# A one-layer decoder step on one core: SyncE issues key pages ahead of value pages in each slot's turn

## The reference

```python
def fox_sample(q, k, v, logf, k_past, v_past, logf_past):
    c = jnp.cumsum(jnp.concatenate([logf_past, logf], axis=1), axis=1)
    s = jnp.concatenate([einsum('bqhd,bkhd->bhqk', q, k_past), einsum('bqhd,bkhd->bhqk', q, k)], -1) * scale
    bias = c[:, p_len:].transpose(0, 2, 1)[..., None] - c.transpose(0, 2, 1)[:, :, None, :]
    p = softmax(where(kpos <= qpos, s + bias, -inf))
    return einsum('bhqk,bkhd->bqhd', p[..., :p_len], v_past) + einsum('bhqk,bkhd->bqhd', p[..., p_len:], v)
...
k_past = cache_k[l][page_table].reshape(bs, past, FOX_HEADS, FOX_HD)
v_past = cache_v[l][page_table].reshape(bs, past, FOX_HEADS, FOX_HD)
```

## Time and profile before

| | |
|---|---|
| time, median of 3 runs (lowest, highest) | 2030.86 us (2027.76, 2032.69) |
| the profiled execution's own time | 2028.18 us |
| its span, first to last instruction | 2026.50 us |
| PE busy | 1946.4 us, 96% of the span |
| DVE, ACT, POOL busy | 56%, 32%, 10% |
| mean granted TensorE clock | 0.990 of full speed |
| cache page loads | 256 of keys and 256 of values, 256 KB each |
| median time from issue to landing of a page | 4.7 us |

### The profile page before, as it was taken

How to read it: one execution, slowest core, us unless ns; L and a number is a source line. 1 busy time by engine, 2 the same in 40 slices (tenths; PEclk the granted TensorE clock), 3 DMA queues, 4 the chain that set the end, 5 groups by cost and what they waited for, 6 DMA issues and landing times.

```text
span 2026.5 us, 37147 instructions
## 1 busy us (share of the span) xinstructions
PE 1946.4 (96%) x14259; PEld 1824.2 (90%) x14259; DVE 1144.4 (56%) x1757; ACT 644.4 (32%) x1202; POOL 196.4 (10%) x230
## 2 busy tenths in 40 slices
PE   7999999999999999989999998999999999999996
PEld 6887888988888898878899997999999999999996
DVE  6545646988877967886426758433323333243348
ACT  5434444234134133223402215433102231132334
POOL 1000000111010020020000100000000000000005
PEclk9999999999999999999999999999999999999999
DMA  5111113898997988887724310111111111111154
GB/s 160 42 43 43 42 43 100 267 309 278 320 314 243 332 284 279 296 294 249 255 80 135 91 42 22 53 42 52 42 52 42 52 39 46 51 42 52 37 158 139
DMA packets 152197, 276.66 MB, mean 137 GB/s; under 512 B 19009, under 2 KB 58702, under 8 KB 152054
## 3 DMA queue, kind: packets, MB, share of 16 engines
q1 hardware_dynamic: 116418, 175.22, 25.8%
q0 software_dynamic: 23296, 82.96, 14.0%
q10 hardware_dynamic: 12368, 16.88, 2.4%
HBM read 247.37 MB, written 27.72 MB: 136 GB/s over the span
## 4 chain that ended last, share of the span: by engine, by line
PE 77%; DVE 12%; DMA 6%; issue 2%; ACT 2%; SPq 2%; ACTq 0%; DVEq 0%; POOL 0%; POOLq 0%
PE bank L125 56%; PE bank L142 5%; PE bank L1788 3%; DMA cache_keys<-in_cache_k_dram 2%; PE bank L983 2%; PE bank L521 2%; PE bank L533 2%; DVE score L1288 2%; DVE cache_keys L1284 1%; DMA cache_vals<-in_cache_v_dram 1%; SPq L845 1%; PE banks L505 1%; PE banks L507 1%; PE banks L1079 1%; DMA x_stage<-in_x_prompt_dram 1%
## 5 line engine op out<-in xcount | busy, mean ns | idle before, releaser
L125 PE MATMUL bank<-x_hi,w_hi 128*128 128x344 f32 x1872 | 608.2, 325 | 7.6 <-DVE rot_sin L1356 3.9
L125 PE MATMUL bank<-x_hi,w_lo 128*128 128x344 f32 x1872 | 599.6, 320 | 0.0
L125 PE MATMUL bank<-x_lo,w_hi 128*128 128x344 f32 x1872 | 599.2, 320 | 0.0
L125 PEld LDWEIGHTS bank<-x_hi,w_hi 128*128 128x128 f32 x1872 | 353.7, 189 | 19.4 <-issue 8.9
L125 PEld LDWEIGHTS bank<-x_lo,w_hi 128*128 128x128 f32 x1872 | 353.3, 189 | 0.2 <-issue 0.2
L125 PEld LDWEIGHTS bank<-x_hi,w_lo 128*128 128x128 f32 x1872 | 353.5, 189 | 0.0
L101 ACT ACTIVATE w_hi<-w_raw 128x1024 fp32r<-128x1024 f32 (+3 forms) x139 | 142.1, 1023 | 380.6 <-PE bank L125 365.8
L125 PE MATMUL bank<-moving_lo,w_hi 128*128 128x344 f32 x744 | 237.5, 319 | 0.0
L125 PE MATMUL bank<-moving_hi,w_hi 128*128 128x344 f32 x744 | 223.1, 321 | 2.4 <-DVE moving_lo L1962 2.0
L108 DVE TENSOR_TENSOR w_lo<-w_raw,w_hi 128x1024 fp32r<-128x1024 f32 (+1 forms) x138 | 164.0, 1189 | 79.9 <-ACT w_hi L101 72.2
L125 PE MATMUL bank<-moving_hi,w_lo 128*128 128x344 f32 x648 | 207.1, 320 | 0.0
(11 more groups left out here) (295 smaller groups left out, 2863.7 us busy)
## 6 DMA issues: line engine op xcount, KB each, us to landing
cache_keys<-in_cache_k_dram SPq DMA_DIRECT2D x256, 256.0 KB, 4.7
cache_vals<-in_cache_v_dram SPq DMA_DIRECT2D x256, 256.0 KB, 4.7
w_raw<-in_w_in_dram POOLq DMA_DIRECT2D x52, 512.0 KB, 6.1
w_raw<-in_w_up_dram POOLq DMA_DIRECT2D x22, 512.0 KB, 4.5
w_raw<-in_w_gate_dram POOLq DMA_DIRECT2D x22, 512.0 KB, 4.6
tail_raw<-in_w_down_dram SPq DMA_DIRECT2D x22, 448.0 KB, 3.7
gate<-gate_t_scratch SPq DMA_DIRECT2D x15, 516.0 KB, 3.5
w_raw<-in_w_down_dram POOLq DMA_DIRECT2D x10, 448.0 KB, 4.4
```

Source lines behind the costliest of these rows:

```text
L125: mm = pe.matmul(g.bank[n][0:m, 0:TC], w[slot][:, k, 0:m], x[:, k, chunk(n)], start=(k == 0 and i == 0), stop=(k == kt - 1 and i == 2))
```

## The change

In `load_both` the two loads of a slot's turn change places: the key group's wait and its two pages come first, the value group's wait and its two pages behind them. The load of the value groups' page numbers moves with them, from before the first turn to between the first key group and the first value group. The functions around it, the rings, the waits' values and all other engines' programs stay as they are.

```diff
             def load_both(n, q, of, quad):
 
-                value_ids = page_ids(of, quad)
+                key_ids = page_ids(n, q)
                 for slot in range(SLOTS):
+                    load_group(keys, k_land, k_used, ck, n, q, slot, key_ids)
+                    if slot == 0:
+                        value_ids = page_ids(of, quad)
                     load_group(vals, v_land, v_used, cv, of, quad, slot, value_ids)
-                    if slot == 0:
-                        key_ids = page_ids(n, q)
-                    load_group(keys, k_land, k_used, ck, n, q, slot, key_ids)
```

## The result

| | kernel before | changed kernel |
|---|---|---|
| time, median (lowest to highest; runs) | 2030.57 us (2025.39 to 2035.04; 6) | 2044.38 us (2039.0 to 2050.28; 6) |
| ratio of the two, 95% interval | | 1.0068 (1.0054 to 1.0083) |
| the profiled execution, its span | 2028.18, 2026.5 us | 2050.28, 2048.6 us |
| mean granted TensorE clock | 0.990 | 0.981 |

The change costs 13.8 us, or 0.68%. Two executions in all, one of the kernel before timed beside runs 1 to 4 (2461.24 us) and one of run 8's kernel timed again (2380.12 us), ran at a mean granted clock of 0.72 and 0.75 and are left out of every median and ratio here. The changed kernel's profiled execution is its slowest, 5.9 us above its median. The two profiles differ by 22.1 us in span, and a share of that is not the change's, as the first windows show.

The account below looks back on a forecast made before the run. TensorE was taken to set the end of the 345 to 1000 us stretch. Terms 2.7 + 2.6 + 1.1 + 1.1 - 1.0 + 3.7 = +10.2 us, added to 2030.86, gave 2041 us, range 2034 to 2054.

Parts of the forecast that it names:

- Head 1's end: Value group 54, issued behind key group 70's wait, lands 3.3 us late near 659 us; +2.7 us, bounds to +6.0.
- the +8 that the prediction names: Approximate sum in us if a 256 KB page took 2.6 us, making groups 54 and 86 each 1.9 us late.
- Head 2's end: Value groups 86 and 89 come 3.0 and 4.8 us late, 2.15 there already; +2.6 us, bounds +0.9 and +5.6.
- Head 0, value group 8: Takes key group 24's place at 429.20 us and lands at most 1.3 us late; +1.1 us, bounds 0 and +2.0.
- The gain at 516 us: Earlier key group 39 shortens TensorE's 3.9 us wait behind VectorE's rotation; -1.0 us, bounds 0 and -1.8.
- Head 3, group 102: TensorE already waits for values here and each is issued one place later; +1.1 us, bounds 0 and +2.0.
- TensorE's clock: New stalls at 659 and 817 us drop the clock to half rate for a while; +3.7 us, bounds +1.0 and +8.0.
- the two terms named as likely to be off: If only the size was wrong, the error was expected in the clock's term or in value group 89's.
- rival 3: Much slower: TensorE's lateness feeds back through VectorE's rotations and key slots at heads 1 to 3; 2055 us, chance 0.05.
- rival 1: Faster: earlier keys make VectorE earlier and remove TensorE's stalls behind it; 2023 to 2024 us, chance 0.08.
- The signs named ahead: Value waits 12 to 20 us, stalls near 659 and 817 of 2.5 to 4, key waits under 33.0, SyncE's over 100.
- The sign of SyncE's queue: SyncE has no value issue between the key groups at 644 and 656 us.

Follow-up runs that it names:

- runs 1 to 4: Keys first except in each sample's second four groups, only there, before's order with key wait first, values one turn ahead: 2041.96, 2040.71, 2041.34, 2034.21 us.
- run 8: Kernel before with values one turn ahead only in groups 4 to 11 of samples 1, 3 and 5: 2027.07 us; timed again, 2028.91 us (11 runs).
- runs 3 and 5: The former: before's page order, each turn first waiting for the key slot, 2041.34 us; the latter: changed kernel with keys two turns ahead, 2078.3 us.
- run 3: Kernel before with its page order kept, each turn first waiting for the key slot its second half needs: 2041.34 us, ratio 1.0060.
- run 4: Kernel before with values one turn further ahead of keys everywhere, the opposite change: 2034.21 us, ratio 1.0016.

## Why the prediction was right, and where its sizes were off

The forecast was 2041 us, the median 2044.38: slower, inside of the range, 3.4 us above. The mechanism is the predicted one. SyncE issues no value group while it stands at key group 70's wait, and runs 3 and 5 show that such waits make a half or more of the loss. Term by term, as idle time of TensorE in the first pair of profiles and, in brackets, in the second:

- **Head 1's end, +2.7 forecast: +4.4 (+4.3).** Group 54 is late by 3.73 (3.79) us where 3.3 was worked out, and the 0.54 (1.22) us of group 57 is swallowed, as foreseen. The landing was 4.98 us from issue to last semaphore where 0.52 + 4.0 = 4.52 had been taken. What is missing in the forecast is group 60, 1.18 (1.77) us. The Trainium skill's page "DMA: Bandwidth & Descriptors", section Anatomy of one DMA, gave an estimate of 2.6 us for a page; the two pages of this group took 4.2 us in the median, and the measurement decides. Carried through all its places, that estimate would have given a sum near +5, not the +8 that the prediction names.
- **Head 2's end, +2.6 forecast: +2.5 (+2.3).** The sum came out, its parts did not, which is luck. Group 86 is late by 3.74 (3.79) us, not 3.0, and group 89's own stall of the earlier trace rows is gone, since TensorE's lateness takes it in. The prediction had let it grow. It had named group 89 as a place where the size might be off.
- **Head 0, value group 8, +1.1 forecast: nothing.** The group lands 1.35 us before TensorE takes it. It took 7.4 us from issue to landing instead of 9.1, and TensorE itself was 1.3 us late.
- **The gain at 516 us, -1.0 forecast: +1.8 (+0.3).** This is the step that failed, in two ways. First, value groups 20 to 22 stall there for 0.65 + 1.07 + 2.02 = 3.74 us (3.95). Second, the gain from earlier keys did not come. TensorE's waits for the rotation fall from 3.91 to 1.99 us (from 3.96 + 0.44 to 0.79), but not because VectorE is sooner. Its two rotations end here at 515.97 + 0.52 and 522.54 + 0.52 us before, and at 523.94 + 0.52 and 530.51 + 0.52 in the changed kernel:

```profile
515.97 0.52 DVE L1359 TENSOR_TENSOR rq_t<-rot_cos,rot_sin 128x344 f32<-128x344 f32 x1
522.54 0.52 DVE L1359 TENSOR_TENSOR rq_t<-rot_cos,rot_sin 128x344 f32<-128x344 f32 x1
```

```profile
523.94 0.52 DVE L1359 TENSOR_TENSOR rq_t<-rot_cos,rot_sin 128x344 f32<-128x344 f32 x1
530.51 0.52 DVE L1359 TENSOR_TENSOR rq_t<-rot_cos,rot_sin 128x344 f32<-128x344 f32 x1
```

  Counted from the stage's start (340.0 and 346.5 us) both are 1.5 us later in the changed kernel, which is about what TensorE is behind by then (the clock's term, below), and VectorE's two waits for keys just ahead of them are 0.96 + 1.84 us before and 1.70 + 1.26 after. The wait of 3.91 us went because TensorE had lost that much at the value groups and came late itself; the 1.99 us are a wait for the second of the two rotations. Head 0's end has the same wait for a key slot as the ends of heads 1 and 2. In the kernel before SyncE issued value group 20 here, and key group 36 when VectorE let go of its slot:

```profile
481.73 0.85 SPq L845 DMA_DIRECT2D cache_vals<-in_cache_v_dram  x2
```

```profile
492.18 1.93 SPq L845 DMA_DIRECT2D cache_keys<-in_cache_k_dram  x2
```

  In the changed kernel:

```profile
499.98 1.97 SPq L845 DMA_DIRECT2D cache_keys<-in_cache_k_dram  x2
502.87 0.85 SPq L845 DMA_DIRECT2D cache_vals<-in_cache_v_dram  x2
```

  Group 20 went out 16.2 us before TensorE wanted it and had landed 12.7 us ahead of its use; in the changed kernel it goes out 2.9 us before, and its followers in a row behind it. The prediction looked at the head's start (group 8) and at its gain, and left the third place of the same kind out. Looking through all key slots that come free late, by the gaps in SyncE's timeline, would have found it.
- **Head 3, group 102, +1.1 forecast: +0.5 (+3.1)** over all of head 3. The new stall is at group 100 (2.10 and 2.86 us), not at 102.
- **TensorE's clock, +3.7 forecast for two stalls: 2.24 + 1.74 = 4.0 us at those two.** The kernel before has 1.04 us of this already, behind its stall of 2.15 us, which the prediction's sum did not take off, so 2.9 are new. In the whole stage the time at half clock grew by 13.7 us (17.1), of which half, 6.8 (8.5) us, is the most that it can cost. Of this 3.4 us (3.4) stand near 415 us, ahead of every new stall: at value group 16 the changed kernel is already 1.3 us behind in both pairs, with the same idle time within 0.2 us. That is no work of the order of loads, as far as the runs tell: run 8's first profile, with the order of before at that point, has as much half clock there (6.8 us) as the changed kernel's first. The rest of the growth, beside the two stalls, stands behind group 100's in the first pair and behind group 60's in the second. The clock was one of the two terms named as likely to be off.

In sum: idle +9.2 by these places (+9.4 over the whole stage; +9.9 in the second pair) instead of +6.5, and for the clock what the stage's difference leaves, 5.3 (6.9) us with those 1.3, instead of +3.7. That the total came within 3.4 us owes something to luck: a stall that was not foreseen, of 3.7 us, is partly offset by a term that came to nothing (+1.1) and by the shorter wait for the rotation, which shrank for another reason than the one given. Two smaller slips of the recorded sums change nothing: 6.61 less 3.97 is 2.64, and rival 3's sum is 20.8 and not over 21, so about 2052 us.

Of rival 1 only VectorE's shorter waits for keys were seen, and they gave TensorE nothing at 516 us. Rival 3's feeding back was not seen: groups 54 and 86 are late by the same 3.7 to 3.8 us, so head 1's lateness didn't add to head 2's. The signs named ahead came out: 18.3 us of waits for values (12 to 20), VectorE's waits for keys 21.4, SyncE's for VectorE over 100. The values' stalls near 659 and 817 were inside of the 2.5 to 4 us. The sign of SyncE's queue holds in substance: group 53 still goes out between the two key groups, at 654.92, and group 54 waits behind the second.

Open stays how much of the loss is the order's and not the wait's (run 3), and the clock ahead of the stage. The part ahead took 339.3 and 340.0 us in the two profiles of before and 340.2 to 346.5 us in the eleven of other kernels, whose code is the same there. Whether that is chance alone or has to do with where a program lies wasn't tried. Nor was it tried how much a single stall costs with no other near it.

## What to carry to other kernels

When one queue issues for two rings, every wait in it holds the loads of both. Put the load for the engine that sets the end ahead of the wait for an engine that doesn't, but not so far that the other engine's waits reach the first (run 4), and price a swap by the slack of each group against the longest standstill of the queue, at **every** place where the freeing engine does something else for a while. A stall that was mended tends to come out at the next group with little slack, and stalls near each other hide one another: parts of such a change don't add up, so try the whole.

## What the runs showed of the hardware

A stall of some 2 us sometimes brought TensorE's clock down to 1.2 GHz and sometimes didn't. In the second profile of the changed kernel it fell right behind the stall of 1.77 us at 695.48; in the first, no stretch at half clock followed that of 2.02 us at 518.72. And code without any change spent different times at half clock: 13.7 us ahead of the stage in both profiles of before, 34.1 and 17.1 in those of the changed kernel, and the same instructions took 339.3 to 346.5 us. A pair of profiles of this kernel can so differ by 7 us ahead of the first changed instruction. A comparison of spans has to be made by stage.
